# One VectorE operation for both halves of a rotary product, in a kernel without its fill matmuls

## The reference, cut to what matters

```python
h = rms_norm(x, g_pre_mix[l])
proj = h @ w_in[l]                       # queries, keys, values, pool input, gates
q = apply_rope(q); k = apply_rope(k)     # in apply_rope:
t1, t2 = tf[..., :half], tf[..., half:]
out = concatenate([t1 * cos - t2 * sin, t2 * cos + t1 * sin], axis=-1)
```

## Time and profile before

| | |
|---|---|
| median of three runs | 994.52 us (993.9 to 994.97) |
| the profiled execution | 994.52 us; span of its slowest core, core 3, 993.0 us |
| spans of the eight cores | 989.5 to 993.0 us |
| TensorE busy | 929.5 us, 94% of the span |
| VectorE, GpSimd, ScalarE busy | 380.8, 364.8, 345.8 us |

### The profile page before, as it was taken

The page is one execution under the profiler, slowest core; times in us unless marked ns, Lnnn a source line. Parts: engine busy times, 40 slices in busy tenths (PEclk is TensorE's granted clock), DMA queues, the critical chain, the costliest instruction groups (busy, mean ns, idle before and its releaser), DMA issues.

```text
span 993.0 us, 15345 instructions; the slowest of 8 cores (989.5 to 993.0 us)
## 1 busy us (share of the span) xinstructions
PE 929.5 (94%) x5574; PEld 474.3 (48%) x5574; DVE 380.8 (38%) x509; ACT 345.8 (35%) x556; POOL 364.8 (37%) x366
## 2 busy tenths in 40 slices
PE   4989998979989999999889999999999999999992
PEld 2456776545554444444444444444444444444441
DVE  5768645677586334334453122111112111221111
ACT  4697446644446224224773111110101111111110
POOL 1528734646576435336882101102331000001322
PEclk9999999999999999999999999999999999999997
DMA  8968801310244334323876576662324444421221
GB/s 231 289 181 242 171 23 44 48 39 1 44 86 86 64 64 128 64 43 105 270 243 166 108 127 119 114 107 64 127 85 128 85 68 81 80 48 36 93 85 42
DMA packets 30778, 105.03 MB, mean 106 GB/s; under 512 B 3952, under 2 KB 3952, under 8 KB 30704
## 3 DMA queue, kind: packets, MB, share of 16 engines
q0 software_dynamic: 14432, 45.65, 27.2%
q1 hardware_dynamic: 15984, 58.33, 17.3%
q10 hardware_dynamic: 288, 0.06, 0.0%
HBM read 132.90 MB, written 16.78 MB: 151 GB/s over the span
## 4 chain that ended last, share of the span: by engine, by line
PE 79%; ACT 5%; POOL 5%; DVE 5%; issue 4%; DMA 1%; POOLq 0%; ACTq 0%; DVEq 0%; SPq 0%
PE ps L637 70%; PE ps L635 10%; DVE PT_75_117 L635 1%; ACT PT_75_117 L635 1%; DMA xst_37_79<-xo 1%; ACT xsb_53_95 L635 1%; POOL x1b_101_143 L635 1%; POOL x1b_102_144 L635 1%; ACT acc_70 L635 1%; POOL x1b_104_146 L635 1%; ACT junk_54_96 L635 1%; POOL x1b_103_145 L635 1%; ACT xsb_52_94 L635 0%; DVE PT_74_116 L635 0%; ACT junk_55_97 L635 0%
## 5 line engine op out<-in xcount | busy, mean ns | idle before, releaser
L637 PE MATMUL ps<-wdna_155,ffT_154 128*128 128x512 bf16 x512 | 115.7, 379 | 0.0
L637 PE MATMUL ps<-hT_68,wgu_109_151 128*128 128x512 bf16 x420 | 100.4, 379 | 0.0
L637 PE MATMUL ps<-hT_68,wgu_110_152 128*128 128x512 bf16 x420 | 100.4, 379 | 0.0
L637 PE MATMUL ps<-hT_68,wgu_111_153 128*128 128x512 bf16 x392 | 93.7, 379 | 0.0
L637 PEld LDWEIGHTS ps<-wdna_155,ffT_154 128*128 128x128 bf16 x512 | 50.1, 98 | 60.4
L637 PEld LDWEIGHTS ps<-hT_68,wgu_109_151 128*128 128x128 bf16 x420 | 41.0, 98 | 49.3
L637 PEld LDWEIGHTS ps<-hT_68,wgu_110_152 128*128 128x128 bf16 x420 | 41.0, 98 | 49.1
L637 PEld LDWEIGHTS ps<-hT_68,wgu_111_153 128*128 128x128 bf16 x392 | 38.3, 98 | 46.3
L637 PE MATMUL ps<-hT_68,wgs_76_118 128*128 128x512 bf16 x224 | 53.6, 379 | 0.6 <-ACT tg_80_122 L635 0.6
L637 PE MATMUL ps<-hT_68,wgs_77_119 128*128 128x512 bf16 x224 | 53.6, 379 | 0.0
L635 DVE TENSOR_TENSOR ffT_154<-ps,sa_115_157 128x512 bf16<-128x512 f32 x30 | 20.7, 691 | 79.2 <-PE ps L635 79.2
(11 more groups left out here) (499 smaller groups left out, 1821.2 us busy)
## 6 DMA issues: line engine op xcount, KB each, us to landing
wgu_109_151<-wgu POOLq DMA_DIRECT2D x15, 512.0 KB, 5.7
wgu_110_152<-wgu POOLq DMA_DIRECT2D x15, 512.0 KB, 5.7
wgu_111_153<-wgu POOLq DMA_DIRECT2D x14, 512.0 KB, 5.6
wgs_76_118<-wg POOLq DMA_DIRECT2D x8, 512.0 KB, 5.5
wgs_77_119<-wg POOLq DMA_DIRECT2D x8, 512.0 KB, 5.2
wdna_155<-wdn POOLq DMA_DIRECT2D x8, 512.0 KB, 8.4
tab_70_112<-tab SPq DMA_DIRECT2D x6, 512.0 KB, 6.0
tab_71_113<-tab SPq DMA_DIRECT2D x6, 512.0 KB, 7.3
```

Source lines behind the costliest of these rows:

```text
L637: e.ops.append(lambda q, m=method, a=a, k=k: getattr(q, m)(*a, **k))
```

## The change

Two edits.

The fill matmuls go: `fill`, its call in `schedule`, `warm`, and the setting of the filler. No other step of the program depends on them.

In `rope` the four VectorE operations become two. Each multiplies both halves of the projection, a PSUM operand of 2 x 512 columns over two banks, by two table halves at once. For the second result the table is read sine first, by a step of -512 between the two halves. The GpSimd operations stay.

```diff
-            if e is self.pe and e.free > 0.0 and t > e.free + 1.0:
-                self.fill(t)
-                t = max(t, e.free)
...
-    def warm(n, vt, count):
-        n.deps.add(d_ident.idx)
-        n.cost = 0.216 * count
-        for _ in range(count):
-            n.items.append(("matmul", (vt[:, :], ident[:, :], fap(ident[:, :], [(0, 4), (1, 128)])), dict(start=True, stop=True)))
-
-    P.filler = (any1, warm)
...
-        cos, sin = tb[:, 0, t0:t0 + n], tb[:, 1, t0:t0 + n]
+        f = tb[:, 0, t0:t0 + n]
         mm8(b[:, 0, 0:n], wa, rhs)
         mm8(b[:, 1, 0:n], wb, rhs)
-        for dst, fa, fb, op in ((dst_a, cos, sin, ALU.subtract), (dst_b, sin, cos, ALU.add)):
+        for dst, swap, op in ((dst_a, False, ALU.subtract), (dst_b, True, ALU.add)):
             t = rt.new()
-            dve.tensor_tensor(out=t[:, 0, 0:n], in0=b[:, 0, 0:n], in1=fa, op=ALU.mult)
-            dve.tensor_tensor(out=t[:, 1, 0:n], in0=b[:, 1, 0:n], in1=fb, op=ALU.mult)
+
+            tf = tb[:, 1, t0:t0 + n].fap([(-512, 2), (1, n)]) if swap else f.fap([(512, 2), (1, n)])
+            dve.tensor_tensor(out=t[:, :, 0:n], in0=b[:, :, 0:n], in1=tf, op=ALU.mult)
             pool.tensor_tensor(out=dst, in0=view(t[:, 0, 0:n]), in1=view(t[:, 1, 0:n]), op=op)
```

More of the change, by code:

```diff
@@ L467, in earliest @@
         return t
[L469 to L489, removed]
     def schedule(self):
@@ L508, in schedule @@
         import bisect
-        left = len(nodes)
-        while left:
+        while len(self.order) < len(nodes):
             pick = None
@@ L533, in schedule @@
             e = n.eng
-            if e is self.pe and e.free > 0.0 and t > e.free + 1.0:
-                self.fill(t)
-                t = max(t, e.free)
-            left -= 1
             e.ready.remove(n)
@@ L834, in build_program @@
     act.dma(small[:, :], small_d[:, :], dsem("d_small"))
-    d_ident = act.dma(ident[:, :], ident_d[:, :], dsem("d_ident"))
+    act.dma(ident[:, :], ident_d[:, :], dsem("d_ident"))
     d_w = [dsem("d_w%d" % i) for i in range(5)]
```

## The result

The changed kernel takes 1006.44 us (median of four runs, 1004.74 to 1007.01) beside 994.33 of the kernel before (993.9 to 994.97): ratio 1.0118, 95% interval [1.0101, 1.0136]. The forecast was 996.8 us, with a range to 1002.0. So the sign was right, the size was not, and the time lies outside the range.

A forecast was written before the change was run, and what follows sets the result against it. It took the tile loop (load, ScalarE, transposes, VectorE) to set the pace up to 62 us, and nearly full TensorE from 78 us, except in the attention. Sum: 994.5 + 0.8 + 1.5 + 0 = 996.8 us, range 990.5 to 1002.

The forecast's parts named there:

- the early gain: Without fills tile 2's transposes no longer wait: 1.7 us gained (1.5 to 2.0) at the first query rope's start.
- the rival of a slow reversed step: Rope operations: reading the table by a step of -512 halves the rate, 1005 us or above; chance 0.05.
- the rival at 991.5: Early wait at tile 6: the planner puts its reciprocal earlier, scaling before 32 us, 990.5 to 993 in all; chance 0.28.
- The rival in which the clock holds: First and second query ropes: the clock stays up without fills, so their removal costs nothing, 993.3 us; chance 0.12.
- 0.3 + 1.5 = 1.8 us: Missing fills: first query rope ends 0.3 us later, cold second rope at 40 us delays ScalarE's chain by 1.5.
- the 0.5 for the merge: First query rope: both merged operations wait for the second half, so GpSimd starts 0.5 us later.
- 0, with -2 to +4: Attention: 16 ropes hold a PSUM pair some 1.1 us longer, against shorter `rt` holding; taken as 0 us.
- 3 us on either side: Whole kernel: the planner's lists may change order anywhere, which no view prices; allowed 3 us either way.
- attention loses too: Attention: a quarter of the longer PSUM hold reaches TensorE in 16 ropes, 4.4 us more, 1001 us; chance 0.17.
- 4.2 at best: All ropes: 60 merged pairs save 0.07 us each, at best 4.2 us of VectorE time, counted at nothing.
- The loads follow the scaling that frees their buffers: DMA loads: not moved by the edits themselves, they shift with ScalarE; no time was given for it.
- A difference that arises after 140 us: Sign of being wrong: TensorE's idle time between 140 and 300 us was to stay the same within 2 us.

The follow-up runs named there:

- e1: The kernel before with its order and four-operation ropes kept, the fills taken out after planning: 997.63 us, 1.0028 against before.
- e11: e1 again on another chip, fills out, order and ropes of before: 996.72 us, 1.0028 against before.
- e3: The changed kernel with fills put back into its finished lists in the first 40 us, four runs: 992.13 us, 0.9973 against before.
- e6: The changed kernel again, unchanged, on another chip: 993.89 us, 0.9999 against before.
- e4: e3 with only the later two runs of fills, ahead of the second query rope: 993.74 us, 0.9990 against before.
- e5: e3 with only the earlier two runs of fills: 994.13 us, 0.9992 against before.
- e18: e1 again on a third chip: 995.67 to 997.85 us in five executions without a low-clock pair, 1011.76 and 1012.72 in two with one.
- e7: e3's lists with each merged operation issued as two of 512 columns, both behind the second half: 0.9977 against before.
- e10: The changed kernel again, unchanged, on another chip: 1005.94 us, 1.0123 against before.
- e14: The changed kernel as marker for the 0.81 clock; markers took 992.9 to 996.3 us without a low-clock pair, 1003.8 to 1006.7 with one.
- e15: The changed kernel without fills, its merged operations split in two as in e7: 1006.49 to 1008.07 us.

## Why the prediction was wrong, point by point

**The early steps came, the early gain did not.** On core 0 of after:

```profile
15.55 0.91 PE L610 MATMUL ps<-ident_43,xsb_52_94 128*128 128x128 bf16 x7 [2.88 <-ACT st_12_54 L608]
...
23.28 2.98 PE L610 MATMUL ps<-hT_68,wq_49_91 128*128 128x512 bf16 x7
...
26.31 1.67 PE L610 MATMUL ps<-hT_68,wq_49_91 128*128 128x512 bf16 x7
...
28.31 1.22 DVE L608 TENSOR_TENSOR rt_72_114<-ps,tab_70_112 128x1024 f32<-128x1024 f32 x1 [3.49 <-PE ps L608]
29.45 1.21 DVE L608 TENSOR_TENSOR rt_73_115<-ps,tab_70_112 128x1024 f32<-128x1024 f32 x1
29.68 1.94 POOL L608 TENSOR_TENSOR q_33_75<-rt_72_114 128x512 bf16<-128x512 f32 x1 [16.64 <-DVE rt_72_114 L608]
...
33.22 1.15 ACT L608 ACTIVATE xsb_52_94<-xst_42_84,st_15_57 128x1024 bf16<-128x1024 f32 x1 [5.73 <-DVE st_15_57 L608]
...
41.22 2.52 PE L610 MATMUL ps<-hT_68,wq_49_91 128*128 128x512 bf16 x7 [0.44 <-DVE hT_68 L608]
...
45.52 0.55 PE L610 MATMUL ps<-ident_43,xsb_53_95 128*128 128x128 bf16 x7
```

Tile 2's transposes start as soon as it is scaled, not behind fills. The first rope starts at 23.28 (forecast 23.3) and cold: its first seven matmuls take 2.98 us against 1.67, six of them 0.43 us apart, where I had nine. The merged operations take 1.22 us, and the reversed one 1.21: the rival of a slow reversed step falls. Tile 6 is scaled at 33.22 (33.9 forecast, 33.07 in the earlier trace rows), so the order did not turn, and the rival at 991.5 falls. The second rope starts cold too, 2.52 us for seven, so about four of them at the half clock, where I had nine again. The rival in which the clock holds falls.

But these times set core 0 of after beside core 3 of before, on which the first rope starts last of all eight. Core 0 of before:

```profile
23.53 1.67 PE L637 MATMUL ps<-hT_68,wq_49_91 128*128 128x512 bf16 x7
...
31.58 1.15 ACT L635 ACTIVATE xsb_52_94<-xst_42_84,st_15_57 128x1024 bf16<-128x1024 f32 x1 [4.22 <-DVE st_15_57 L635]
```

On the median of the eight cores the first rope starts at 23.6 us in before and at 23.8 in after, so the gain of 1.7 us that I had read from core 3 isn't there; on core 3 itself it is 1.0 (24.00 against 25.02). Tile 6 is scaled at 31.6 and 33.6, 2.0 us later where I had 0.8.

**The fills: right in kind, somewhat small.** I had 0.3 + 1.5 = 1.8 us for them, without the 0.5 for the merge. They cost 2.5 to 2.9 (e1, e11, e3 to e6). The early half weighs as much as the late one: e4, without the early fills, takes 1.6 us more than e3, where I had 0.3, and e5, without the late ones, 2.0, where I had 1.5. The median core shows it as well: its last transposes come at 106.1 in before and at 108.6 to 109.7 in e1, e11 and e18. I also left out that all eight cores count, and the slowest sets the time: without fills the cores lie 3.5 to 5.5 us apart at that landmark (2.8 with them in before, but 7.0 with them in e3, so the fills aren't all of it).

**The merge: its later start was a small term, the order a large one.** Counted at 0.5 us in stage 1 and "0, with -2 to +4" in the attention, it took 5.2 us out of the middle (409.5 to 404.3, all cores alike). That is the term that was sized wrong beside the clock's: I had allowed the order 3 us on either side in words, and the bounds of the sum held only -2. The rival "attention loses too" had the wrong sign. VectorE itself saves more than I had read, 7.7 us of busy time and not 4.2 at best, as two of the four operations of a rope had run by themselves and not back to back; e7 shows that this doesn't reach the time.

**A load that I moved and didn't price.** "The loads follow the scaling that frees their buffers" stood in the prediction, at nothing. In the new order ScalarE takes the square-sum of the sixth halo tile ahead of the scalings of two tiles that are already there. On core 1 of after:

```profile
59.26 1.11 POOL L608 DMA_DIRECT2D wk_67_109<-wk  x2
60.53 0.33 SPq L608 DMA_DIRECT2D xsth_44_86<-xh  x1
...
68.59 1.06 ACT L608 ACTIVATE junk_55_97<-xsth_44_86 128x1024 bf16<-128x1024 f32 x1 [1.96 <-DMA xsth_44_86<-xh]
...
69.94 1.13 ACT L608 ACTIVATE xsb_53_95<-xsth_47_89,st_13_55 128x1024 bf16<-128x1024 f32 x1
70.98 1.13 ACT L608 ACTIVATE xsb_52_94<-xsth_48_90,st_12_54 128x1024 bf16<-128x1024 f32 x1
```

The load is issued at 60.53, when its buffer is free, and lands 8.0 us later; the core's 16 DMA engines are nearly idle up to 62 us (a share of 0.05 from 60 to 62) and full from then on (0.97 from 62 to 78). ScalarE waits 1.96 us with two scalings queued behind. In before those two scalings stand ahead of it in ScalarE's list, and the square-sum at 67.25 finds its tile there; core 3:

```profile
56.24 1.10 POOL L635 DMA_DIRECT2D wk_67_109<-wk  x2
60.44 0.33 SPq L635 DMA_DIRECT2D xsth_44_86<-xh  x1
...
65.17 1.13 ACT L635 ACTIVATE xsb_53_95<-xsth_47_89,st_13_55 128x1024 bf16<-128x1024 f32 x1
66.21 1.13 ACT L635 ACTIVATE xsb_52_94<-xsth_48_90,st_12_54 128x1024 bf16<-128x1024 f32 x1
67.25 1.04 ACT L635 ACTIVATE junk_55_97<-xsth_44_86 128x1024 bf16<-128x1024 f32 x1
```

ScalarE's order alone is the smaller part: it is ready for the tile at 66.63 in after and at 67.25 in before. The load itself has become slower. From issue to landing it takes 3.8 to 5.1 us on the eight cores of before and 3.6 to 6.1 in e1, but 5.4 to 9.6 in after, e3 and e6, the kernels with the new order. GpSimd's two weight loads now come just ahead of it, at 59.26 and not at 56.24; that they are what slows it is likely but not shown. In e6 cores 0, 3, 4 and 7 wait 2.3 to 3.6 us for a halo load, and their last transposes come at 110.5 to 112.6; core 5 waits 0.9 (109.8); cores 1, 2 and 6 have no such wait (107.2 to 108.1). The worst, core 4's ScalarE from 40 to 108 us (us in all, times, longest):

```profile
ACT junk L608 <- DMA xsth<-xh: 3.6, 1, 3.6
```

In before three cores wait for a halo load, at most 2.4 us in all, in e1 one, 1.6 us; in e3, which has the fills and the new order, six cores wait, up to 3.5 us. So of the 5.2 us won in the middle some 2 to 3 seem to have gone here, on the slowest cores; 2.6 remained.

**The step that failed: what a cold start can cost.** The prediction let each rope's cold start be over within its sixteen matmuls, at most 1.8 us for the first and 3.0 for the second. All its cases had a clock of 0.50 or 1.00, falling when TensorE idles and rising when it works. What decided instead was a third level after the rise, 0.81 for about 160 us on two to six cores. "A difference that arises after 140 us" stood among the signs that would make me wrong, and it came: on a core at 0.81 the middle takes 414.5 to 416.3 us where its neighbours take 404.3, 10 to 12 us more, and stage 1 ends up to 2 us later (114.3 against 112.3), together the 12 us between 993.9 (e6) and 1005.9 (e10). No view of the kernel before shows this level in its profiled execution, so a range from its rows alone could not price it; but of eight cores that all restart from cold together I could have asked what the chip does, and I costed one core. That the forecast had the right sign is luck: without that stretch the changed kernel is no slower than before (e6, 0.9999).

Without that stretch the time is 993.9, 2.9 us below the forecast. Two steps separate what is in it: the missing fills cost 2.6 us (e3 to e6), and the merge with its order gave 2.6 (before to e3). In the second the middle gave some 5 us, and stage 1 took about half of it back; how the slower load and the merge's later start share that isn't separated.

## What to carry to other kernels

Fill matmuls that look like padding kept eight TensorEs from starting cold: before removing them, ask not only what the cold start costs on one core, but what the granted clock does afterwards, and look at every core of several executions on more than one chip. (That it matters that the cores rise together is a guess that no run here tests.) A change that alters a planner's cost or dependence changes the order everywhere; here that was worth -5 to +10 us in the middle of the kernel, more than either edit costs without the 0.81, and only keeping the lists fixed while changing the instruction (and the other way round) tells them apart. Two landmarks per core turn a span into stages, and a stage that is constant to 0.2 us in all kernels leaves the search small.

## What was not expected of the hardware

The stretch at 0.81 has a length of its own. On 16 cores (six of after, six of e10, two of e14, two of e15) it starts at 47.75 to 51.0 us and ends at 207.75 to 210.0, read in quarter microseconds: 158.75 to 161.5 us on each (on 11 of them with a short spell at the half clock inside it), although TensorE works on as densely afterwards. It comes to both cores of a pair, never to one alone, and to one to three pairs of the four in an execution; the two of a pair fall within 0.25 us of each other, and in the trace's own records of the clock they keep it equally long, to 0.01 us (161.52 us on cores 4 and 5 of after, 159.38 on cores 2 and 3). The matmul's time fits: 2.01 us for seven against 1.67.

The Trainium skill, in "TensorE: Matmul & The Clock Gate", Part 1, tells of a peak-current limiter that takes a whole die to 13/16 of the clock, 0.8125, once three of its cores run dense matmuls, and holds it there while the load lasts. The level agrees with the 0.81 of these rows. For this stretch the rest doesn't: it takes pairs, lets go after 160 us under the same load, and the kernel before runs eight cores at a granted 1.00 nearly throughout (mean clocks 0.986 to 0.988). So the measurement decides, and whether it is that limiter at all isn't shown.

A table read backwards by a step of -512 costs nothing (1.21 us against 1.22). A 1024-column operation over two PSUM banks saves 0.07 us against two of 512 back to back (1.22 against 1.29), and e7 shows that this saving is worth nothing where VectorE has idle time.
